# Whole-precision products for the first 32 output-projection units of the even attention

## What is computed

```python
    o_nsa = nsa_attention(q_n, k_cmp, v_cmp, k_slc, kv_n[:, :, 3], k_win, kv_n[:, :, 5], gates, rel_bias[:, :NSA_HEADS])
    ...
    o_mla = mla_attention(q_nope, q_pe, k_nope, k_pe, kvf[..., MLA_NOPE:])
    return jnp.concatenate([o_nsa, o_mla], axis=-1) @ w_out
```

## Time and profile before

| what | us |
|---|---|
| median of three runs | 2056.01 |
| the profiled execution, first to last instruction (span) | 2054.0 |
| PE busy | 1889.3 |
| DVE busy | 1559.5 |
| ACT busy | 1057.0 |
| POOL busy | 220.1 |

### The profile page before, as it was taken

How to read it: one execution, slowest core, us unless ns; L and a number is a source line. 1 busy time by engine, 2 the same in 40 slices (tenths; PEclk the granted TensorE clock), 3 DMA queues, 4 the chain that set the end, 5 groups by cost and what they waited for, 6 DMA issues and landing times.

```text
span 2054.0 us, 34033 instructions
## 1 busy us (share of the span) xinstructions
PE 1889.3 (92%) x11434; PEld 1629.2 (79%) x11434; DVE 1559.5 (76%) x2447; ACT 1057.0 (51%) x2257; POOL 220.1 (11%) x317
## 2 busy tenths in 40 slices
PE   3279998889999999999999999989999999999998
PEld 2158854766799999997877878777799999998787
DVE  4988744777778888889887888788677777778554
ACT  1145446655544545555544456565455555556443
POOL 2220001552100000000011000043000000000000
PEclk9689998999999999999999999999999999999999
DMA  8979985567588888886997886868567777765555
GB/s 325 399 278 320 339 295 170 198 229 245 200 278 281 270 273 277 278 272 231 331 332 266 271 282 203 301 220 300 193 232 224 225 234 235 224 203 177 177 189 176
DMA packets 210967, 521.25 MB, mean 254 GB/s; under 512 B 23041, under 2 KB 43010, under 8 KB 186018
## 3 DMA queue, kind: packets, MB, share of 16 engines
q1 hardware_dynamic: 180722, 316.19, 47.3%
q0 software_dynamic: 28032, 201.44, 26.9%
q10 hardware_dynamic: 2096, 2.12, 0.3%
HBM read 517.53 MB, written 2.12 MB: 253 GB/s over the span
## 4 chain that ended last, share of the span: by engine, by line
PE 73%; DVE 13%; DMA 9%; ACT 3%; issue 1%; SPq 0%; DVEq 0%; POOLq 0%; ACTq 0%
PE ps L1039 12%; PE ps L1035 12%; PE ps L1036 12%; PE ps L931 10%; PE ps L927 10%; PE ps L928 10%; DVE acc L1712 6%; DVE ring_lo L1790 3%; DMA ring<-in_od_w_in 2%; DMA first_ring<-in_ada_w 2%; DMA ring<-in_ev_w_in 1%; DMA aring<-in_ada_w 1%; PE ps L761 1%; PE ps L1131 1%; DVE L L1947 1%
## 5 line engine op out<-in xcount | busy, mean ns | idle before, releaser
L1242 ACT ACTIVATE ring_hi<-ring 128x512 fp32r<-128x512 f32 (+2 forms) x1152 | 690.8, 621 | 595.5 <-DMA ring<-in_ffn_w_up 231.6
L1790 DVE TENSOR_TENSOR ring_lo<-ring,ring_hi 128x512 fp32r<-128x512 f32 (+2 forms) x1152 | 742.3, 680 | 283.1 <-ACT ring_hi L1242 281.4
L1035 PE MATMUL ps<-hT_hi,ring_hi 128*128 128x256 f32 x2048 | 512.2, 283 | 1.5 <-PE ps L1039 0.7
L1036 PE MATMUL ps<-hT_lo,ring_hi 128*128 128x256 f32 x2048 | 507.2, 280 | 0.0
L1036 PEld LDWEIGHTS ps<-hT_lo,ring_hi 128*128 128x128 f32 x2048 | 387.3, 189 | 0.0
L1035 PEld LDWEIGHTS ps<-hT_hi,ring_hi 128*128 128x128 f32 x2048 | 384.7, 188 | 2.3 <-issue 1.2
L1039 PE MATMUL ps<-hT_hi,ring_lo 128*128 128x256 f32 x2048 | 329.2, 282 | 2.4 <-DVE ring_lo L1790 2.4
L1039 PEld LDWEIGHTS ps<-hT_hi,ring_lo 128*128 128x128 f32 x2048 | 279.2, 187 | 2.6 <-DVE ring_lo L1790 2.6
L1712 DVE SCALAR_TENSOR_TENSOR acc<-aring,cs,acc 128x2048 f32<-128x2048 f32 x112 | 263.4, 2352 | 20.6 <-DMA aring<-in_ada_w 8.8
L928 PE MATMUL ps<-ring_hi,hT_lo 128*128 128x512 f32 (+2 forms) x640 | 243.8, 382 | 0.0
L643 POOL DMA_DIRECT2D aring<-in_ada_w x176 | 94.4, 536 | 1380.7 <-DVE acc L1712 1355.6
(11 more groups left out here) (244 smaller groups left out, 1996.4 us busy)
## 6 DMA issues: line engine op xcount, KB each, us to landing
aring<-in_ada_w POOLq DMA_DIRECT2D x176, 1024.0 KB, 6.9
ring<-in_ffn_w_up SPq DMA_DIRECT2D x512, 256.0 KB, 3.0
ring<-in_ffn_w_down SPq DMA_DIRECT2D x256, 256.0 KB, 3.1
ring<-in_od_w_in SPq DMA_DIRECT2D x112, 256.0 KB, 3.5
ring<-in_ev_w_in SPq DMA_DIRECT2D x80, 256.0 KB, 5.8
first_ring<-in_ada_w POOLq DMA_DIRECT2D x16, 1024.0 KB, 7.2
ring<-in_ev_w_out SPq DMA_DIRECT2D x64, 256.0 KB, 3.5
ring<-in_od_w_out SPq DMA_DIRECT2D x64, 256.0 KB, 4.0
```

Source lines behind the costliest of these rows:

```text
L1035: nc.tensor.matmul(o[q], hi, hT_hi[:, kt, :], start=start, stop=False, skip_group_check=True)
L1036: nc.tensor.matmul(o[q], hi, hT_lo[:, kt, :], start=False, stop=False, skip_group_check=True)
L1242: ins = nc.scalar.activation(out_, in_, f, **kw)
L1790: put(v.tensor_tensor(ring_lo[:, g, part], ring[:, g, part], ring_hi[:, g, part].bitcast(F32), ALU.subtract), lo_ok)
```

## The change

`ev_out` joins the native matrices with its first 32 units. These are no longer rounded by ACT nor subtracted by DVE. The products of the attention become `whole`: the raw head `hT` by the raw unit of `ring`, both float32, two matmuls for a unit instead of six. They wait for `o_out` and for the load. As `hT_lo` overwrites `hT`, the remainder of a head now waits until PE has used the head's second unit, and it moves from 5 to 9 steps after the head's last unit of work; DVE's loop is four steps longer. `heads_out` still uses the split parts of the heads and waits for the remainders: for 11 of them before its first part, for all 16 before the second. The odd attention keeps what it had.

```diff
-NATIVE = "ev_mid"
+NATIVE = {"ev_mid": 52, "ev_out": 2 * KT}
...
+        native += NATIVE.get(name, 0)
         plan[name], skipped[name] = at, native
         at += n
-        native += n if name == NATIVE else 0
...
                 for q, b in products_at(att, n):
-                    pe.wait_ge(att.o_lo.handle, q + 1)
+                    if att is ODA:
+                        pe.wait_ge(att.o_lo.handle, q + 1)
                     product(q, b)
...
+                def whole(q, b):
+
+                    kt, at = att.kt[q], 2 * q + b
+                    g = PLAN[name] + at
+                    pe.wait_ge(att.o_out.handle, q + 1)
+                    wait_unit(g)
+                    for t in range(ST):
+                        ins = nc.tensor.matmul(ps[:, 2 * b + t, :], hT[:, kt, t * P:(t + 1) * P], ring[:, g % RING, :],
+                                               start=q == 0, stop=q == KT - 1)
+                    lane.done(ins, unit_used)
+
...
-                return product
+                return whole if name in NATIVE else product
...
                 gate_rows(n, range(0, 2))
+                if att is EVA:
+                    pe.wait_ge(att.o_lo.handle, 11)
                 rows_block(name, 2 * KT, KT, NB, 4, left, part=(0, 6))
                 pe.wait_ge(gate_ok.handle, 4 * n + 2)
+                if att is EVA:
+                    pe.wait_ge(att.o_lo.handle, KT)
                 gate_rows(n, range(2, 4))
...
                     q = head_at(att, n, SPLIT_AT)
-                    if q is not None:
+                    if q is not None and name not in NATIVE:
                         highs(name, 2 * q, 2 * q + 2)
...
                 def remainder(n):
 
-                    q = head_at(att, n, LAG + 2)
+                    q = head_at(att, n, PRODUCT_AT + 3 if name in NATIVE else LAG + 2)
                     if q is not None:
                         dve.wait_ge(att.o_hi.handle, q + 1)
+                        if name in NATIVE:
+                            dve.wait_ge(unit_used.handle, PLAN[name] + 2 * q + 2)
...
-                for n in range(len(units) + LAG + 3):
+                for n in range(len(units) + (PRODUCT_AT + 4 if name in NATIVE else LAG + 3)):
...
                     q = head_at(att, n, SPLIT_AT + 1)
-                    if q is not None:
+                    if q is not None and name not in NATIVE:
                         lows(name, 2 * q, 2 * q + 2)
```

## The result

The changed kernel took 2083.67 us (median of four runs, 2083.12 to 2087.28) against 2056.32 for the kernel before on the same chip: ratio 1.0136, 95% interval 1.0114 to 1.0158. It is slower by 27 us, and the forecast of 2057.3 us and its range up to 2062.0 were wrong.

A forecast was written before the change was run, and what follows sets the result against it. PE was taken as the bound (busy 92% of the span), its gaps in the even attention closed by DVE. Periods -4.6, hand-over +4.6 and low clock +1.3 sum to +1.3 on 2056.0: 2057.3 us, range 2052.2 to 2062.0.

The forecast's parts named there:

- the frame of the sum: Whole kernel: only the even attention and the hand-over behind it, about 340 to 493 us, were taken to change.
- The products, +1.17 a period: Even attention, PE: a unit costs 1.72 us as two full-precision products, adding 1.17 us a period.
- B: Window (win) step of a period, three weight units; start forecast at +6.57 instead of +7.97 us, lasting 7.12.
- The relief, and periods of 16.02: Even attention: DVE drops a split pair, 1.40 us less; periods fall from 16.8 to 16.02, six give -4.6 us.
- C: Compressed (cmp) step of a period, following B; forecast to start 7.12 us after B and take 2.33 us.
- D: MLA step that opens each period; forecast to follow C after 2.33 us, D to D about 16.0 us.
- The hand-over, +4.6 and +1.3: End of even attention: load-paced accumulations delay the block's first low part to +28.9, costing 4.6 us, low clock 1.3.
- The clock's term: Behind the hand-over's new PE wait: one stretch at granted clock 0.50, costing +1.3 us, between 0 and twice that.
- Slow landing: Rival: loads landing in 8.5 us make PE wait in periods (4.8 us) and at the end; 2064.9 us, chance 0.20.
- Fast landing: Rival: loads landing in 5.1 us leave only +0.8 us at the attention's end; 2052.2 us, chance 0.20.
- cheap products: Rival: a full-precision product is one record of 0.43 us, a unit saves 0.5 us; 2047 us, chance 0.04.
- The price by passes: Even attention's products: four passes per full-precision product give 1.88 us a unit, six periods together 3.8 us slower.

The follow-up runs named there:

- e1: Changed kernel with 32 already satisfied waits (16 instructions) ahead of DVE's first wait, restoring DVE's code position; 2074.38 us, ratio 1.0085 to the kernel before.
- e4: Kernel before, computation untouched, with 480 and 258 satisfied waits ahead of DVE's and PE's code, imitating the changed kernel's loop positions; 2076.85 us, ratio 1.0103.
- e3: Changed kernel with both paddings, 16 instructions on DVE and 127 on PE, so both loops stand where they stood before; 2063.91 us, ratio 1.0022.
- f3: Kernel before, splits and waits kept, but the 32 units' six reduced products replaced by two full-precision ones, loop positions kept; 2060.45 us, ratio 1.0022.
- f1: Changed kernel with both loops back in place and the accumulations of steps 39 and 41 moved behind the block's first low parts; 2053.45 us, ratio 0.9980.
- f2: As f1, with the third accumulations of attention steps 8, 16 and 24 moved into the even layer's input projection; 2058.58 us, ratio 1.0003 to the kernel before.
- g5: As f2, but only the 8 NSA heads' units use raw full-precision products; MLA heads keep split and six reduced products; 2051.07 us, ratio 0.9969 to before.
- e2: Changed kernel with 254 already satisfied waits (127 instructions) ahead of PE's first wait, restoring PE's code position; 2075.39 us, ratio 1.0086 to the kernel before.

## Why the prediction was wrong, point by point

**The step that failed is the frame of the sum.** "The change touches only the even attention and the hand-over to the block behind it" counted what instructions do and not where they stand. 16 instructions fewer on DVE and 127 fewer on PE (in the whole span 33858 instead of 34033, the other 32 being ACT's) moved two loops to where their code is fetched again in each pass: +14.6 and +10.5 us, the larger part of the miss. No term and no rival had it; e1 to e4 show it from both sides. Had both loops kept their place, the time would have been 1.0022 of before (e3), about 2060.8 us, inside the range.

**The products, +1.17 a period: right.** A unit took 1.72 us (the three of B 5.32 us with the modelled last record, (5.32 - 0.59) / 11 = 0.43 a record), and f3 shows 0.93 on the path, as counted.

```profile
376.81 5.32 PE L963 MATMUL ps<-ring,hT 128*128 128x512 f32 x12
```

**The relief, and periods of 16.02: right in mechanism, off by 0.2.** With the clock high the six took 97.30 against 96.1: B starts at +6.76 instead of +6.57, C follows after 7.19 instead of 7.12, D after 2.39 instead of 2.33. PE's wait before B fell from 1.74 to 0.21. The term was then -3.4 us instead of -4.6. Of the path by PE's own work, forecast at +6.31, this wait leaves +6.55: PE came 0.24 later than forecast, and DVE, which still releases B, 0.19.

**But in the profiled run the gain was 0: a low clock inside the periods.** The prediction said that such a stretch "inside the end of the attention would hide behind DVE". It took no such stretch inside the periods into the sum. Before, it cost nothing there: 3.41 us at half the clock from 386.6 fell into a period of 16.56, as long as the next of the shorter kind, which had none (16.55). After, PE is 97% busy and nothing hides it: the periods with such a stretch (from 369.7 and 420.9 us) took 17.52 and 17.57, where e3 has 16.02 and 16.36. The period with DVE's wait of 2.57 us for a load ahead of a third accumulation took 17.15 (e3: 16.34), most of the rest.

```profile
420.90:424.30 3.40, 3.40 (x15) 3.22 (x15) 3.21 (x6) 2.08 (x7) 0.00 (x0) 0.50 0.47 195
...
415.38 2.35 DVE L1728 SCALAR_TENSOR_TENSOR acc<-aring,cs,acc 128x2048 f32<-128x2048 f32 x1 [2.57 <-DMA aring<-in_ada_w]
```

Before, one stretch stood in the periods and one behind them, at 482.2; after, both stand in the periods. What brings them there is open: in the 10 us ahead of each, PE's longest marked gap was 0.62 us.

**The hand-over, +4.6 and +1.3: right mechanism and place, mis-sized.** It measured +10.2 (gate rows 0.3 earlier, gate halves 10.55 longer). In us from the last D step, the third accumulation began at +13.2 (forecast 12.85), the fourth at +18.2 (16.05), the fifth at +23.6 (22.6), the sixth at +29.0 (25.8); the low part came at +31.3, and PE took it at +32.0 instead of +28.9. The fourth is the step: its load was to be issued at 8.95, but POOL was in a scaling of 3.83 us until 479.4 and issued at +10.3, and it then took 7.8 us to land instead of 7.1. POOL's own queue was left out of that line. The sixth, which needs the fourth's slot, came 8.2 us after its issue at 489.86. The wait was 7.92, not 5.2. The clock's term was one stretch of 3.41 us; it became 10.24 us, of which 5.1 lay inside the wait (from 496.0 to 501.05) and the rest cost 2.6 us, twice the 1.3. f1 shows that all of it hangs on the two accumulations of steps 39 and 41.

**The rivals.** Slow landing had the sign: its price in the periods, a load landing behind the first accumulation, was there but small: f2 leaves at most 0.25 us for a third accumulation, and the worst in the changed kernel's run was the 0.8 of the period of 17.15. Fast landing did not come up, and cheap products are excluded by f3. None was near 2083. (The range's upper edge, half of 4.8 and all of 2.8 over 2057.3, adds up to 2062.5 and not 2062.0; that changes nothing.)

**The price by passes.** The Trainium skill's four passes (FP8 and Floating Point Precision, TensorE Precision Notes) gave 1.88 us a unit; the measured 1.72 decides for the rows. That full precision costs more than the three reduced products is what the trace shows, 1.72 against 1.41 us a unit.

## What to carry over

An edit that adds or drops instructions ahead of a hardware loop can cost more in that loop than it changes where it stands: compare the instruction packets of the page before and after, and look at each loop's first operation for a wait by "issue" (on PE it can carry another engine's name); where it appears, idle instructions in front of the program can give the time back, here 16 on DVE and 127 on PE. When a kernel's loop is lengthened for one purpose, ask what else rides in it: the two accumulations of the added steps cost 10.5 us at a place where their loads are the pace. And an engine's relief is worth taking only where another engine waits for it: splitting the work unit by unit (g5) gained where the change as a whole did not.

## What the hardware showed that was not expected

- A backward branch to code no longer held (by the packets) stopped DVE for 6.6 to 9.1 us (e2, after) and PE for 2.4 to 3.1 us (e4, e1) a pass; through PE's waits and the low clock that came with them it cost the kernel 4.8 to 7.3 us for each such pass in up0 (e4, after; the 7.3 with the stretch at 577.9 us in it) and 4.0 to 5.5 in up1 (e4, e1).
- The named releaser misled there: PE's wait of 2.63 us at 1703.34 is put down to ACT's `ring_hi`, and it went away by padding PE alone (e2). At the same place in e1 the stop, 3.13 us at 1686.47, is put down to "issue".
- During or right behind PE's waits of 2.63, 3.36, 5.65 and 7.92 us above the granted clock was 0.5 for 3.41 to 10.24 us. A gap alone doesn't tell it: one of 2.35 us in up0 before had no such stretch and one of 2.36 us after had, and two stretches stood in the periods with no gap over 0.62 us ahead. While PE has slack a stretch of 3.41 us cost nothing (the period of 16.56 before); when it had none, 1.2 to 1.5 us of a period (17.57 against 16.36, 17.52 against 16.02).
